# The first 56 microseconds of a two-block network kernel: zeros multiplied at the start, the first load split, and the first head's small groups placed five dense steps later

## What is computed

```
proj = h @ w_in                                # h = rmsnorm(x, g)
qkv, gate, a_raw, b_raw = split(proj)
qkv = silu(causal_dwconv(qkv, conv_w))         # 4 taps
q, k, v = split(qkv); q, k = l2norm(q), l2norm(k)
g = -exp(a_log) * softplus(a_raw + dt_bias); beta = sigmoid(b_raw)
G = cumsum(g); decay = exp(G_i - G_j)          # causal
tri = strict(beta * (k k^T) * decay) + I       # solved per chunk and head
u, w = solve(tri, v * beta), solve(tri, k * beta * exp(G))
# then a scan over the chunks of a head, with state S
```

## Time and profile before

| | value |
|---|---|
| median of three runs | 1310.2 us (1309.98 to 1310.95) |
| the profiled execution | 1310.99 us, its span 1309.2 us |
| PE busy in the span | 1286.1 us (98%) |
| PEld, DVE, ACT busy | 83%, 73%, 53% |
| mean granted PE clock | 0.998 |
| DMA | 119.5 MB, mean 91 GB/s |

### The profile page before, as it was taken

The page is one execution under the profiler, slowest core; times in us unless marked ns, Lnnn a source line. Parts: engine busy times, 40 slices in busy tenths (PEclk is TensorE's granted clock), DMA queues, the critical chain, the costliest instruction groups (busy, mean ns, idle before and its releaser), DMA issues.

```text
span 1309.2 us, 24374 instructions
## 1 busy us (share of the span) xinstructions
PE 1286.1 (98%) x9309; PEld 1087.2 (83%) x9309; DVE 958.3 (73%) x1543; ACT 690.2 (53%) x1100; POOL 16.5 (1%) x16
## 2 busy tenths in 40 slices
PE   7999999999999999999999999999999999999998
PEld 5788888888788998989987777788888989899876
DVE  7778778875767877777767877775777777777655
ACT  6666676765563434444346666733634344343452
POOL 0000000000000000000011000000000000000100
PEclk9999999999999999999999999999999999999999
DMA  4232322322234332323232222234243332332232
GB/s 163 79 91 62 75 80 65 81 66 81 80 98 138 96 121 96 97 96 98 67 95 81 65 65 64 65 90 119 81 159 96 101 96 96 97 97 86 77 94 97
DMA packets 40733, 119.52 MB, mean 91 GB/s; under 512 B 3984, under 2 KB 11600, under 8 KB 40656
## 3 DMA queue, kind: packets, MB, share of 16 engines
q1 hardware_dynamic: 33184, 114.78, 28.4%
q10 hardware_dynamic: 7472, 3.70, 1.8%
HBM read 116.34 MB, written 2.13 MB: 90 GB/s over the span
## 4 chain that ended last, share of the span: by engine, by line
PE 89%; DVE 6%; ACT 2%; issue 2%; DMA 1%; SPq 0%; DVEq 0%; ACTq 0%
PE acc L429 12%; PE acc L430 11%; PE acc L431 11%; PE ps L873 6%; PE ps L871 6%; PE ps L872 6%; PE acc L856 4%; PE acc L855 4%; PE ps L856 4%; PE acc L854 4%; PE ps L854 4%; PE ps L855 4%; DVE work L2414 1%; DVE wl L405 1%; PE ps L989 1%
## 5 line engine op out<-in xcount | busy, mean ns | idle before, releaser
L429 PE MATMUL acc<-xh,wh 128*128 128x512 f32 x624 | 260.0, 417 | 9.4 <-DVE xl L2595 8.4
L430 PE MATMUL acc<-xl,wh 128*128 128x512 f32 x624 | 245.5, 394 | 0.0
L431 PE MATMUL acc<-xh,wl 128*128 128x512 f32 x624 | 245.5, 393 | 0.0
L405 DVE TENSOR_TENSOR wl<-raw,wh 128x1024 fp32r<-128x1024 f32 x111 | 135.9, 1226 | 49.9 <-ACT wh L398 47.8
L429 PEld LDWEIGHTS acc<-xh,wh 128*128 128x128 f32 x624 | 118.3, 190 | 35.6 <-DVE wl L405 9.5
L431 PEld LDWEIGHTS acc<-xh,wl 128*128 128x128 f32 x624 | 118.1, 189 | 25.9
L430 PEld LDWEIGHTS acc<-xl,wh 128*128 128x128 f32 x624 | 118.6, 190 | 21.1 <-issue 1.2
L398 ACT ACTIVATE wh<-raw 128x1024 fp32r<-128x1024 f32 x111 | 115.7, 1048 | 29.1 <-DMA raw<-in_weights 19.7
L1495 ACT ACTIVATE wh<-raw 128x1024 fp32r<-128x1024 f32 x48 | 50.9, 1061 | 110.9 <-PE ps L856 110.9
L856 PE MATMUL acc<-yh,wl 128*128 128x512 f32 x256 | 99.9, 390 | 0.0
L855 PE MATMUL acc<-yl,wh 128*128 128x512 f32 x256 | 99.8, 390 | 0.0
(11 more groups left out here) (354 smaller groups left out, 2907.8 us busy)
## 6 DMA issues: line engine op xcount, KB each, us to landing
raw<-in_weights SPq DMA_DIRECT2D x208, 512.0 KB, 3.6
work<-rows ACTq DMA_DIRECT2D x14, 256.0 KB, 6.9
h<-in_xT SPq DMA_DIRECT2D x4, 512.0 KB, 6.2
outT<-h SPq DMA_DIRECT2D x8, 256.0 KB, 2.5
cst<-in_cst SPq DMA_DIRECT2D x1, 512.0 KB, 5.8
work<-in_pT SPq DMA_DIRECT2D x1, 512.0 KB, 4.7
kept<-in_keep SPq DMA_DIRECT2D x1, 208.0 KB, 5.8
work<-in_w_ab SPq DMA_DIRECT2D x1, 128.0 KB, 7.1
```

Source lines behind the costliest of these rows:

```text
L405: nc.vector.tensor_tensor(lo[:], raw[u.const % 2][:], hi[:].bitcast(F32), ALU.subtract).then_inc(lo_done, 1)
L429: nc.tensor.matmul(dst[:], hi, mh[:, k, :], start=(n == 0), stop=False)
L430: nc.tensor.matmul(dst[:], hi, ml[:, k, :], start=False, stop=False)
L431: mm = nc.tensor.matmul(dst[:], lo, mh[:, k, :], start=False, stop=(n == KT - 1))
```

## The change

It does five things, all in the first block's start.

1. DVE sets the tile `M(4)` to zero first of all, and PE multiplies it with itself four times (128x512, plain float32) into bank `ps[5]` before its first real product.
2. Unit 0 is loaded and split in two halves of 128x512; the first tile of the input is loaded alone, between them; `keep` is loaded after unit 1.
3. The squares are made in four instructions of two tiles, and added in three adds of two tiles and one of one tile.
4. Every small group from the second on stands later in PE's order: sums after 14 steps in place of 10, all others five steps later; `START_STEPS` is 47 in place of 42 and `FIRST_FILL` has 25 steps in place of 30.
5. The product for q of head 0 (unit 2) goes to `ps[5]`, and unit 4 waits for one evacuation of its bank fewer.

```diff
+            if u.per == 0 and u.const == u_q(0).const:
+                return ps[5]
             return acc[u.const % 2]
...
-                pe.wait_ge(evac[b], u.half(-2 if beside else 0))
+                pe.wait_ge(evac[b], u.half(-2 if beside else -1 if u.per == 0 and u.const == 4 else 0))
...
             sp.dma_start(par[:, 0:NPAR], a["params"]).then_inc(s_par, 16)
-            load_unit(sp, 0, 0)
-            for n in range(4):
-                sp.dma_start(h[:, 2 * n:2 * n + 2, :],
-                             a["xT"].rearrange("(k p) t -> p k t", p=P)[:, 2 * n:2 * n + 2, :]).then_inc(s_x[n], 16)
-                if n == 1:
-                    sp.dma_start(keep[:], a["keep"]).then_inc(s_keep, 16)
+            tiles = a["xT"].rearrange("(k p) t -> p k t", p=P)
+            sp.dma_start(raw[0][:, 0:T].unsqueeze(1), a["weights"][:, 0:1, 0:T]).then_inc(w_first, 16)
+            sp.dma_start(h[:, 0:1, :], tiles[:, 0:1, :]).then_inc(x_first, 16)
+            sp.dma_start(raw[0][:, T:].unsqueeze(1), a["weights"][:, 0:1, T:]).then_inc(w_in[0], 16)
+            sp.dma_start(h[:, 1:2, :], tiles[:, 1:2, :]).then_inc(s_x[0], 16)
+            for n in range(1, 4):
+                sp.dma_start(h[:, 2 * n:2 * n + 2, :], tiles[:, 2 * n:2 * n + 2, :]).then_inc(s_x[n], 16)
             sp.dma_start(W(21)[:, 0:2 * P], a["w_ab"]).then_inc(s_wab, 16)
             load_unit(sp, 1, 1)
+            sp.dma_start(keep[:], a["keep"]).then_inc(s_keep, 16)
             sp.dma_start(cst[:, 0:5 * 16], a["levels"]).then_inc(s_cst, 16)
...
-        FIRST_FILL = [3, 3, 0, 2, 3, 2, 3, 2, 1, 1, 1, 2, 1, 2, 2, 2]
+        FIRST_FILL = [2, 2, 0, 2, 2, 2, 2, 2, 1, 2, 1, 2, 1, 1, 1, 2]
...
         def pe_start(pe, todo):
+            pe.wait_ge(zp, 1)
+            for _ in range(4):
+                nc.tensor.matmul(ps[5][:], M(4)[:, 0:P], M(4), start=True, stop=True)
...
-                pe.wait_ge(x_sq, KT - 1)
+                pe.wait_ge(x_sq, 4)
...
-        START_AT = [8, 10, 12, 15, 18, 20, 21, 29, 31, 33, 34, 36, 37, 39, 41]
-        START_STEPS = 42
+        START_AT = [8, 14, 17, 20, 23, 25, 26, 34, 36, 38, 39, 41, 42, 44, 46]
+        START_STEPS = 47
...
-            split_hi(act, Unit(0))
+            act.wait_ge(w_first, 16)
+            nc.scalar.activation(wh[0][:, 0:T], raw[0][:, 0:T], ACT.Copy).then_inc(first_hi, 1)
...
-            for k in range(KT):
-                nc.scalar.activation(W(11 + k), h[:, k, :], ACT.Square).then_inc(sqs, 1)
+            for n in range(4):
+                nc.scalar.activation(two_tiles(11 + 2 * n), h[:, 2 * n:2 * n + 2, :], ACT.Square).then_inc(sqs, 2)
...
+            nc.vector.memset(M(4), 0.0).then_inc(zp, 1)
             nc.vector.memset(xpad[:, 0:3], 0.0).then_inc(zp, 1)
...
-            for k in range(1, KT):
-                dve.wait_ge(sqs, k + 1)
-                if k > 1:
-                    dve.wait_ge(x_sq, k - 1)
-                nc.vector.tensor_tensor(accb, W(11) if k == 1 else accb, W(11 + k), ALU.add).then_inc(x_sq, 1)
+            for n in range(1, 4):
+                dve.wait_ge(sqs, 2 * n + 2)
+                if n > 1:
+                    dve.wait_ge(x_sq, n - 1)
+                nc.vector.tensor_tensor(W(11, 2), W(11, 2), W(11 + 2 * n, 2), ALU.add).then_inc(x_sq, 1)
+            dve.wait_ge(x_sq, 3)
+            nc.vector.tensor_tensor(accb, W(11), W(12), ALU.add).then_inc(x_sq, 1)
```

More of the change, by code:

```diff
@@ L418, in unit_steps @@
             b, (whi, wlo), dst = u.const % 2, slot(u), accumulator(u)
-            pe.wait_ge(lo_done, u.number(1))
+            if not u.known_below(1):
+                pe.wait_ge(lo_done, u.number(1))
             if not u.known_below(2) and dst is acc[b]:
                 beside = u.per == 0 and u.const in (U_OUT1 + 6, U_OUT1 + 7)
-                pe.wait_ge(evac[b], u.half(-2 if beside else 0))
+                pe.wait_ge(evac[b], u.half(-2 if beside else -1 if u.per == 0 and u.const == 4 else 0))
             for n, k in enumerate(order):
@@ L1730, in _ @@
             act.preload_act_table_set(LN_EXP)
-            split_hi(act, Unit(0))
+            act.wait_ge(w_first, 16)
+            nc.scalar.activation(wh[0][:, 0:T], raw[0][:, 0:T], ACT.Copy).then_inc(first_hi, 1)
             act.wait_ge(s_par, 16)
             for k in range(KT):
-                if k % 2 == 0:
+                if k == 0:
+                    act.wait_ge(x_first, 16)
+                elif k == 1:
+                    act.wait_ge(w_in[0], 16)
+                    nc.scalar.activation(wh[0][:, T:], raw[0][:, T:], ACT.Copy).then_inc(hi_done, 1)
+                    act.wait_ge(s_x[0], 16)
+                elif k % 2 == 0:
                     act.wait_ge(s_x[k // 2], 16)
@@ L1829, in dve_take_head @@
                 dve.wait_ge(tap3_d, at)
-            nc.vector.tensor_tensor(xpad[:, 3:3 + T], acc[u.const % 2][:], xrstd, ALU.mult).then_inc(evac[u.const % 2], 1)
+            nc.vector.tensor_tensor(xpad[:, 3:3 + T], accumulator(u)[:], xrstd, ALU.mult).then_inc(evac[u.const % 2], 1)
         def dve_gate(dve, j):
@@ L2589, in _ @@
         def _(dve):
+            nc.vector.memset(M(4), 0.0).then_inc(zp, 1)
             nc.vector.memset(xpad[:, 0:3], 0.0).then_inc(zp, 1)
-            split_lo(dve, Unit(0))
+            dve.wait_ge(first_hi, 1)
+            nc.vector.tensor_tensor(wl[0][:, 0:T], raw[0][:, 0:T], wh[0][:, 0:T].bitcast(F32), ALU.subtract).then_inc(first_lo, 1)
             dve.wait_ge(s_par, 16)
             for k in range(KT):
+                if k == 1:
+                    dve.wait_ge(hi_done, 1)
+                    nc.vector.tensor_tensor(wl[0][:, T:], raw[0][:, T:], wh[0][:, T:].bitcast(F32), ALU.subtract).then_inc(lo_done, 1)
                 dve.wait_ge(xh_done, k + 1)
```

11 lines of the change are left out of this document (9 added, 2 removed).

## The result

The changed kernel takes 1315.66 us (median of six, 1311.04 to 1316.88); the kernel before took 1310.48 beside it (1309.98 to 1311.21). The ratio is 1.003, with a 95% interval from 1.002 to 1.0041: **slower by 0.3%**, where 1308.7 was forecast, and above the range. (By the means of the six runs each it is 1.003, by the medians 1.004.) The profiled execution took 1314.76 us with a span of 1312.9, 3.7 us longer than the span before, 1309.2. In the rows of the changed kernel L429 to L431 of before are L436 (xh,wh), L437 (xl,wh) and L438 (xh,wl), the sums are L790, the low split L409, the take L1854, the broadcast loads of rows L1200, tx(0) L636 and L653, tx(2) L645, the third mask L1939.

What follows compares the result with a forecast made beforehand. PE, busy 98% of the span, was taken as the bound, meeting ACT's and DVE's chain at tx(2) of period 1. Two steps (-1.37 us) and the chain (-0.2) gave -1.55 us: 1308.7 us, range 1306.9 to 1311.0.

Steps and rivals of the forecast that it cites:

- Zeros: PE's start: products end near 7.6, clock up at 6.8; PE kept from step 0 for 1 to 2 us, covered.
- Order of the loads: Start: last input tiles and unit 1 land 0.53 us earlier, last xl ends near 12.8, unit 0 at 13.5.
- Squares and adds: Unit 1's split to sums: four squares end at 17.2, adds at 19.9, sums at 20.04, 0.60 us earlier.
- Waits of units 3 and 5: Between sums and x(0) of period 1: PE waits 0.6 us for unit 3 and 0.2 us for unit 5.
- tx(0): Period 1: starts at 61.0 on DVE's full queue; PE does two steps before it and idles 2.7 us for 1.9.
- Rows hold tx(2), PE's lead is paid back: Period 1: rows land at 67.1, tx(2) at 73.2; PE idles 1.6 us, three of its five steps lost.
- From tx(2) to period 2: End of period 1: 15 steps in place of 17, two steps or 1.37 us less; period 2 starts at 91.5.
- Nothing later asks for absolute time: From period 2 on: starting at 91.5 for 93.0, later work is bound to no fixed time, so the gain stays.
- a stall that I missed: Anywhere: an unforeseen stall, given only the rest of the chance after cases of 0.55, 0.17, 0.18 and 0.07.
- The second fall of the clock: Rival at tx(2) of period 1: 1.6 us idle brings a fall costing 1.75 us; +0.2, 1310.4; chance 0.18.
- The signs: Wrong if sums before 19.5 or after 21, L636 without wait, period 2 before 90.5, or later periods over 35.5.

Runs made afterwards that it cites:

- e1: Kernel before plus DVE's memset and the four products of zeros alone; 1312.51 us, ratio 1.001.
- e2: Changed kernel without the four products of zeros and the wait on them (memset stays); 1317.96 us, ratio 1.005.
- e10: Kernel before with each head's row loads issued some microseconds earlier on ScalarE, nothing else; 1312.36 us, ratio 1.001.
- e13: Kernel before with the earlier row loads (as e10) and the four products of zeros; 1310.60 us, ratio 0.9995.
- e7: Kernel before with the load of keep moved behind unit 1, nothing else; 1310.45 us, ratio 0.9993.
- e8: Kernel before with unit 0 and the first pair of tiles loaded in two pieces each, keep left in place; 1311.82 us, ratio 1.0005.
- e4: Changed kernel with one step in place of two ahead of tx(0) of period 1 and three in place of two behind it; 1313.89 us, ratio 1.003.
- e6: Kernel before with a short tail: three steps of period 1's fill moved from behind v(2), v(3), os(2) to before; 1313.68 us, ratio 1.0015.
- e9: Changed kernel with each head's row loads issued some microseconds earlier on ScalarE; 1309.56 us, ratio 0.999.
- e11: Kernel before with keep late, squares and adds in pairs, rows early, six steps of unit 5 ahead of tx(0); 1307.50 us, ratio 0.9981.
- e5: Changed kernel where ACT issues period 1's last row loads only after DVE's low part of unit 10; 1316.15 us, ratio 1.0031.
- e12: The combined kernel e11 plus the four products of zeros; 1307.68 us, ratio 0.997.

## Why the prediction was wrong

Taken by its own steps, for the profiled execution:

- **Zeros.** From 1.46 to 7.6, clock up at 6.42: right, and so was that they are worth nothing at the sums (e1, e2). Wrong was that this is all. They are also 16 entries in a stream that comes in blocks of 256, and that decides by microseconds further on (e10 to e13).
- **Order of the loads: the mis-sized term at the start.** 0.53 us earlier by `keep` is what e7 measures. The two extra pieces were costed by their bytes and so at nothing; e8 measures 1.06 us later. The last `xl` ended at 14.26 for 12.8 and unit 0 at 15.3 for 13.5. Together unit 1 landed 0.88 later instead of 0.53 earlier: 1.41 us, and all of it arrives at the sums (21.49 for 20.04, 1.45).
- **Squares and adds.** 6.84 us from the first square to the sums for 6.87: 0.03 where 0.07 was forecast. ScalarE's page of the Trainium skill (ScalarE: Activation LUTs, Rules for kernel authors) would have had 1.2 us in the squares; the row of 3.89 us for four, 0.37 less than for eight, bears the sum by rows out, not that rule.
- **Waits of units 3 and 5.** Forecast 0.6 and 0.2, found 0.38 and 0.16 idle, at 31.63 and 50.01, on L409 and L1854 as named. Right in kind, but they cost more than their idle time: the groups on either side of them are 0.65 us (30.29 to 32.44, for 29.38 to 30.88) and 0.40 us (48.51 to 50.87, for 46.95 to 48.91) further apart. That is 1.05 of the 1.13 us by which sums to x(0) is longer, for 0.8 forecast.
- **tx(0): a step that I missed.** I counted two steps between x(0) and tx(0) and priced them at 0.68 us each. The second is the first of unit 6, which before stood behind tx(0) and had time. It waited until 61.75, and by e4 that cost 0.56 us. tx(0) came at 63.33 for 61.0: 1.45 from the loads, 0.56 from this, and 0.3 between sums and x(0), the waits just told. The stretch to tx(2) had 0.81 of its clock for 0.90.
- **Rows hold tx(2), PE's lead is paid back.** Right only where PE comes early: in e7 and e1 it idles there by 1.5 and 2.2 us, with decay started by the landing. In the kernel before and in the changed one decay didn't wait for the rows, which had landed 0.42 and 0.18 us earlier (66.95, 69.43); it followed ACT's own queue, and that had waited for PE's vtr (until 65.83 and 68.08). The changed kernel idled 0.55, on L1939, at 75.58 for 73.2; being late itself, it had little to pay back.
- **From tx(2) to period 2.** 18.23 us for 19.61: the two steps, 1.38 for 1.37 forecast. So the gain of the change is there, and period 2 starts 0.81 late only since tx(2) is 2.19 late: 0.85 at the sums, 1.13 from there to x(0), 0.21 from x(0) on.
- **"Nothing later asks for absolute time": the step that failed.** It cost 3.2 us. I looked at waits that the trace of before names, and a block of instructions isn't one as long as it comes in time. It was just in time, with 0.26 us idle in the kernel before: e6 shows that the short tail alone, by which the weights are issued 1.4 us later against x(0) and the rows 0.6, makes 2.4 us idle, and e9, that moving the row loads out of its way gives period 2 back. The prediction kept 3% or less for "a stall that I missed", which was too little.
- **The second fall of the clock.** It came, but not where I had it: none followed the 0.55 us at tx(2). The first, while PE waited for unit 6, is that of before (61.04 for 61.71) but lasted 6.8 us for 3.4; the second came behind the stall of period 2 (105.41).
- **The signs.** Of those named for being wrong two came, the sums after 21 (21.49) and a period longer than 35.5 (39.07).

The page on the runtime in the Trainium skill (Runtime: NRT & Kernel Launch, Instruction fetch mechanics) says that instructions lie in a small memory of each engine, are refilled in blocks of 16 KiB by a DMA queue of its own, and that crossing a block is mostly hidden. The trace agrees on the size, 16,384 bytes a packet, and for most blocks on the hiding; the gap of 1.97 us here, up to 3.66 in e2, is where it isn't hidden.

**What stays open.** The profile shows when a block starts, not when it was asked for. That it is PE's follows from the counts of entries, and fits PE's resumption 2.2 to 2.5 us behind it at each of the gaps after 1985 and 2241 entries (3.8 in e2's first, whose block took 2.2 us in place of 0.9). Each kernel was profiled in one execution. Why pieces of 256 KB cost a microsecond wasn't taken apart (the number of loads, or their shorter rows); SP issues the last input pair 0.70 us later in e8 (4.55 for 3.85), but whether the landing follows the issue isn't shown. Nor is it shown why the clock falls behind one idle time and not behind another as long (below). And the six executions of the changed kernel spread over 5.8 us; that the fast one, 1311.04, had its block in time is likely from e11's two groups, but only one of them was profiled.

## What to carry to other kernels

When a kernel with a long unrolled stream has an idle PE under "issue" in the middle of a group, look for the packet of instructions that starts some 2.4 us before PE goes on, and at which data transfers stand ahead of it; spread large loads, or issue them so that a block doesn't stand behind two of them. Count the entries: here such gaps came only at places 256 entries apart. Anything that changes the number of instructions or PE's lead by a microsecond can move such a stall in or out, so a small edit's time is its own only if two neighbours of it (another place for the loads, some entries more) give the same. And dense steps put in a gap must be of a unit that is already there: six of unit 5 ahead of tx(0) removed an idle 1.9 us, one of unit 6 added some.

## What the runs showed of the hardware that was not expected

- A 16 KB block of instructions stood behind data of other queues: it started 9.6 us behind the issue of the rows in e10 (86.48 to 96.05), 9.9 in e11 (82.94 to 92.81). PE stood for 1.5 to 3.2 us behind it, and 3.7 in e2. Once started it took 0.92 to 0.95 us there, 2.19 before e2's first stall.
- PE stood still for instructions only after 1217, 1985 or 2241 entries of its stream, 256 or 3 x 256 apart, in ten kernels (gaps of over 0.25 us under "issue").
- With the rows 0.15 us ahead of the weights for 1.2 the block still came 0.5 us before the last of these data (e5); whether it was asked for before them did matter (e10 against e13, e11 against e12).
- The first loads landed about 1 us later when 1 MB of them was issued as four pieces for two (e8, 11.14 to 12.20 for the last input pair), with 331 GB/s from 3 to 8 for 363.
- 1.9 us idle at tx(0) were followed by a low clock in the kernel before and by none in e7, where the clock stayed up from 11.68 to the end; 2.43 us idle before the sums brought a fall in e12, 1.06 us none in e11. The same idle time can do either: 2.74 us before the sums brought a fall in e13 and 2.73 us none in e1, which runs the same products up to there; at tx(1) of period 2 2.37 us brought one in e6 and 2.48 us none in e4.
- A wait of PE cost more than its idle time in the profile: 0.65 us for 0.38 and 0.40 for 0.16, by the distance between the groups around it.
